# Layer 0's first attention heads: two of sixteen items begun inside the value projections

## What is computed

```python
s1 = jnp.einsum('bqhd,bkhd->bhqk', q1, k1).astype(jnp.float32) * scale
s2 = jnp.einsum('bqhd,bkhd->bhqk', q2, k2).astype(jnp.float32) * scale
a = jax.nn.softmax(s1, axis=-1) - lam * jax.nn.softmax(s2, axis=-1)
return jnp.einsum('bhqk,bkhe->bqhe', a.astype(v.dtype), v)
```

## Time and profile before

| | |
|---|---|
| median of 3 runs | 2467.47 us (2466.74 to 2468.09) |
| the profiled execution | 2467.12 us |
| its span, first to last instruction | 2465.3 us |
| TensorE busy | 2333.8 us, 95% of the span |
| VectorE / ScalarE / GpSimd busy | 1538.9 / 950.7 / 343.7 us |
| mean granted TensorE clock | 0.982 of full speed |

### The profile page before, as it was taken

One profiled execution on the slowest core, in us unless ns is written; L12 is line 12 of the kernel. 1 busy time (PEld: TensorE's weight loads), 2 busy tenths in 40 slices (PEclk: granted clock), 3 DMA queues, 4 the chain that ended last, 5 costly groups with the idle time before them and its releaser, 6 DMA issues.

```text
span 2465.3 us, 33152 instructions
## 1 busy us (share of the span) xinstructions
PE 2333.8 (95%) x13146; PEld 1893.8 (77%) x13146; DVE 1538.9 (62%) x2481; ACT 950.7 (39%) x1768; POOL 343.7 (14%) x455
## 2 busy tenths in 40 slices
PE   6989898999999899999999999999999999999997
PEld 3866566888887778777878787888887778788886
DVE  3647586666667652466778775655574667765457
ACT  4426453422212521476352232322342764433333
POOL 0110101101012210100100313133111110100131
PEclk9999999999999999999999999999999999999999
DMA  6430015654444222110412332333122104332221
GB/s 260 129 117 1 18 58 182 221 180 165 164 145 149 99 69 79 67 61 1 171 64 86 103 133 90 109 131 120 60 77 77 36 2 154 137 119 87 103 86 69
DMA packets 79178, 257.58 MB, mean 104 GB/s; under 512 B 5680, under 2 KB 10416, under 8 KB 70576
## 3 DMA queue, kind: packets, MB, share of 16 engines
q1 hardware_dynamic: 65024, 205.01, 24.2%
q0 software_dynamic: 12704, 46.14, 5.4%
q10 hardware_dynamic: 1296, 4.30, 0.4%
HBM read 246.00 MB, written 9.44 MB: 104 GB/s over the span
## 4 chain that ended last, share of the span: by engine, by line
PE 76%; DVE 12%; ACT 4%; issue 3%; DMA 2%; POOL 1%; SPq 1%; POOLq 0%; DVEq 0%; ACTq 0%
PE PS L1255 9%; PE PS L1257 9%; PE PS L1256 9%; PE PS L1326 5%; PE PS L1328 5%; PE PS L1327 5%; PE PS L1132 4%; PE PS L1151 3%; PE PS L1171 3%; PE PS L977 3%; PE PS L980 3%; PE PS L978 3%; PE PS L1025 1%; PE PS L1224 1%; PE PS L1227 1%
## 5 line engine op out<-in xcount | busy, mean ns | idle before, releaser
L1255 PE MATMUL PS<-HH,WH 128*128 128x512 f32 (+1 forms) x1088 | 420.4, 386 | 9.2 <-DVE TMP L2521 4.6
L1256 PE MATMUL PS<-HL,WH 128*128 128x512 f32 (+1 forms) x1088 | 416.7, 383 | 0.0
L1257 PE MATMUL PS<-HH,WL 128*128 128x512 f32 (+1 forms) x1088 | 416.7, 383 | 0.0
L2708 ACT ACTIVATE WH<-STG 128x1024 fp32r<-128x1024 f32 (+1 forms) x202 | 196.7, 1022 | 279.9 <-PE PS L1328 244.7
L2317 DVE TENSOR_TENSOR WL<-STG,WH 128x1024 fp32r<-128x1024 f32 (+1 forms) x202 | 241.6, 1237 | 36.9 <-ACT WH L2708 36.9
L1326 PE MATMUL PS<-WH,AH 128*128 128x512 f32 x600 | 238.0, 397 | 16.7 <-DVE LOW L2417 5.9
L1255 PEld LDWEIGHTS PS<-HH,WH 128*128 128x128 f32 x1088 | 204.5, 188 | 53.6 <-issue 5.7
L1328 PE MATMUL PS<-WH,AL 128*128 128x512 f32 x600 | 236.2, 394 | 0.0
L1327 PE MATMUL PS<-WL,AH 128*128 128x512 f32 x600 | 235.9, 393 | 0.0
L1257 PEld LDWEIGHTS PS<-HH,WL 128*128 128x128 f32 x1088 | 204.5, 188 | 40.3
L1256 PEld LDWEIGHTS PS<-HL,WH 128*128 128x128 f32 x1088 | 204.6, 188 | 40.0 <-issue 1.0
(11 more groups left out here) (268 smaller groups left out, 4464.5 us busy)
## 6 DMA issues: line engine op xcount, KB each, us to landing
STG<-in_w_up SPq DMA_DIRECT2D x66, 1024.0 KB, 6.0
ADAW<-in_w_ada SPq DMA_DIRECT2D x96, 512.0 KB, 3.8
STG<-in_w_down SPq DMA_DIRECT2D x20, 1024.0 KB, 5.7
ADAW<-in_w_ada POOLq DMA_DIRECT2D x32, 512.0 KB, 4.0
STG<-in_w_ffn_out SPq DMA_DIRECT2D x10, 1024.0 KB, 6.2
STG<-in_ev_w_in SPq DMA_DIRECT2D x8, 1024.0 KB, 5.0
STG<-in_w_in SPq DMA_DIRECT2D x6, 1024.0 KB, 6.9
spill<-X POOLq DMA_DIRECT2D x10, 512.0 KB, 5.1
```

The costliest lines, as they stand in the source:

```text
L1255: e.matmul(out, h_, hh, start=c == 0, stop=False)
L1256: e.matmul(out, h_, hl, start=False, stop=False)
L1257: return e.matmul(out, l_, hh, start=False, stop=c == 7)
L2708: return e.activation(dst, src, ACT.Copy)
```

## The change

- On TensorE the attention object is made before the projections. The second pair of values gets banks 4 and 5, the third 6 and 7, which leaves 0 to 3 to the scores. After the second pair TensorE waits for the last turned query and key (`keys_ready`) and does the scores of item 0; between the two halves of the third pair it does the scores of item 1. The loop starts at item 2, after the wait for the last value copy.
- VectorE does maxima and mix of items 0 and 1 after the second value pair, ScalarE their four exponentials, ahead of the copies of the third pair. Both loops start at item 2.
- Rows 0 to 3 go to X (`a_place`), since HT is still in use. Rows from 4 on keep their places in HT.
- `mix` takes both reciprocals of an item in one instruction over two columns; `total_inverse` is no longer called for A.
- VectorE's wait for the factor NLT moves ahead of the projections.

```diff
+    def a_place(self, n):
+
+        if n < 4:
+            o = (0, 768, 4096, 4864)[n]
+            return self.X[:, o:o + 768]
+        return self.att[0]["HT"][:, n % 6 * 768:(n % 6 + 1) * 768]
...
     def project(L):
         have, late = {v for v in range(2) if turned_ahead(L, v)}, []
         hh, hl = k.ht(L)
+        values = unit_pairs(0, 4) if L == 0 else []
...
+                if pair in values[1:]:
+                    rot["set"], rot["n"] = ([4, 5], [6, 7])[values.index(pair) - 1], 0
                 bs = [take(("proj", L, x[0])) for x in pair]
...
                         turn_late(L, late[:1] if kind == "qa" else late)
+                        if pair in values[2:]:
+                            first_heads.scores(1)
+                if pair in values[1:2]:
+                    keys_ready(0)
+                    first_heads.scores(0)
...
-        def turn(self, i, at, nkt, ready):
+        def scores(self, i):
+            QT, KT = k.reg(0, 0, 2048, 4), k.reg(0, 2048, 5120, 4)
+            h, c = i // 4, i % 4 * P
+            self.score_pair(i, [full_mm(QT[64 * s:64 * s + 64, h, c:c + P], KT[64 * s:64 * s + 64, h, :]) for s in range(2)])
+
+        def turn(self, i, nkt, ready):
             T = PS[:, 6:8, :].rearrange("p b n -> p (b n)")
-            Pt = self.HT[:, at * 768:at * 768 + nkt * P]
+            Pt = k.a_place(2 * i)
...
+    first_heads = PairAtt("A", 0, 6, 2)
...
-    scores_ready(0)
+    for x in values_done(k, 0):
+        w.wait_ge(*x)
...
-    for i in range(16):
...
+    for i in range(2, 16):
+        first_heads.scores(i)
         if i >= 3:
-            a.out_one(i - 3, lambda c, h=(i - 3) // 4: V[:, c, h * P:(h + 1) * P])
-        if i >= 2:
-            a.turn(i - 2, 2 * (i - 2) % 6, 6, k.dv_p(("A", i - 2)))
+            first_heads.out_one(i - 3, values_of(i - 3))
+        first_heads.turn(i - 2, 6, k.dv_p(("A", i - 2)))
...
@@ vector_program
                 step(bg, int(2 <= n < 10))
                 n += 1
+                if pair == unit_pairs(0, 4)[1]:
+                    for i in range(2):
+                        first_maxima(i)
+                        mix(i)
...
-        e.reciprocal(r2, tb).then_inc(*k.dv_rstd.up(("A", i, "r2")))
-        w.wait_ge(*k.dv_rstd(("A", i, "r2")))
+        both = k.small("att", 2 * i, 0, 8).rearrange("p (n j) -> p n j", n=2)
+        e.reciprocal(both[:, :, 2], both[:, :, 1]).then_inc(*k.dv_rstd.up(("A", i)))
+        w.wait_ge(*k.dv_rstd(("A", i)))
...
-    for i in range(18):
+    for i in range(2, 18):
         if i < 16:
-            w.wait_ge(*k.pe_score(("A", i)))
-            for n in (2 * i, 2 * i + 1):
-                largest("A", n, 768)
-        if 1 <= i <= 16:
+            first_maxima(i)
+        if 3 <= i <= 16:
             mix(i - 1)
-            total_inverse("A", 2 * (i - 1))
-        if i >= 2:
-            a_tail(i - 2)
+        a_tail(i - 2)
...
@@ scalar_program
+                if pair == unit_pairs(0, 4)[1]:
+                    w.wait_ge(*k.pe_turn((0, last_turn(0))))
+                    w.wait_ge(*k.pl_kr((0, 11)))
+                    for n in range(4):
+                        power("A", 0, n, 768, n)
                 late = pair
...
-    for i in range(16):
+    for i in range(2, 16):
         for n in (2 * i, 2 * i + 1):
-            if i >= 3:
+            if i >= 5:
                 w.wait_ge(*(k.dv_p(("A", i - 3)) if n % 2 else k.pe_pt(("A", i - 3, 1))))
```

More of the change, by code:

```diff
@@ L998, in project, with keys_ready @@
                 turn(L, x[0], *x[2:])
-    def scores_ready(L):
+    def keys_ready(L):
         us = [u for u, *_ in UNITS[L] if has_turn(L, u)]
@@ L1004, in scores_ready @@
         w.wait_ge(*k.dv_turned((L, [u for u in us if turned_by_dve(L, u) or UNITS[L][u][2] == "b"][-1])))
+    def scores_ready(L):
+        keys_ready(L)
         for s in values_done(k, L):
@@ L1420, in tensor_program, with values_of @@
     step(bg, 8)
-    a = PairAtt("A", 0, 6, 2)
-    QT, KT, V = k.reg(0, 0, 2048, 4), k.reg(0, 2048, 5120, 4), k.reg(0, 5120, 8192, 6)
-    for i in range(16):
-        h, tt = i // 4, LAT[i % 4]
-        a.score_pair(i, [full_mm(QT[64 * s:64 * s + 64, h, (tt - 2) * P:(tt - 1) * P], KT[64 * s:64 * s + 64, h, :])
-                         for s in range(2)])
+    V = k.reg(0, 5120, 8192, 6)
+    def values_of(i):
+        return lambda c: V[:, c, i // 4 * P:(i // 4 + 1) * P]
+    for i in range(2, 16):
+        first_heads.scores(i)
         if i >= 3:
-            a.out_one(i - 3, lambda c, h=(i - 3) // 4: V[:, c, h * P:(h + 1) * P])
-        if i >= 2:
-            a.turn(i - 2, 2 * (i - 2) % 6, 6, k.dv_p(("A", i - 2)))
-    a.out_one(13, lambda c: V[:, c, 3 * P:4 * P])
+            first_heads.out_one(i - 3, values_of(i - 3))
+        first_heads.turn(i - 2, 6, k.dv_p(("A", i - 2)))
+    first_heads.out_one(13, values_of(13))
     for i in (14, 15):
-        a.turn(i, 2 * i % 6, 6, k.dv_p(("A", i)))
-        a.out_one(i, lambda c: V[:, c, 3 * P:4 * P])
+        first_heads.turn(i, 6, k.dv_p(("A", i)))
+        first_heads.out_one(i, values_of(i))
     e.drain().then_inc(*k.pe_end.up("A"))
@@ L2111, in largest, with first_maxima @@
         e.tensor_reduce(k.small("att", n), k.scores(name, n)[:, 0:nk], AX.X, ALU.max, negate=True).then_inc(*k.dv_max.up((name, n)))
+    def first_maxima(i):
+        w.wait_ge(*k.pe_score(("A", i)))
+        for n in (2 * i, 2 * i + 1):
+            largest("A", n, 768)
     def lowest(s, table, start, out):
@@ L2127, in mix @@
     def mix(i):
[L2129 to L2132, removed]
+        ta, r2, rho = k.small("att", 2 * i, 1), k.small("att", 2 * i + 1, 2), k.small("att", 2 * i + 1, 3)
+        pa, pb = k.a_place(2 * i), k.a_place(2 * i + 1)
         w.wait_ge(*k.ac_exp(("A", 2 * i + 1)))
-        e.reciprocal(r2, tb).then_inc(*k.dv_rstd.up(("A", i, "r2")))
-        w.wait_ge(*k.dv_rstd(("A", i, "r2")))
+        both = k.small("att", 2 * i, 0, 8).rearrange("p (n j) -> p n j", n=2)
+        e.reciprocal(both[:, :, 2], both[:, :, 1]).then_inc(*k.dv_rstd.up(("A", i)))
+        w.wait_ge(*k.dv_rstd(("A", i)))
         e.tensor_scalar(rho, r2, ta, k.NLT[:, 0:1], ALU.mult, ALU.mult).then_inc(*k.dv_rstd.up(("A", i, "rho")))
@@ L2613, in vector_program @@
     bg = ada(1, 4)
+    w.wait_ge(*k.dv_lam("neg"))
     project(0, bg)
-    w.wait_ge(*k.dv_lam("neg"))
     def a_tail(i):
@@ L2872, in power @@
         w.wait_ge(*k.dv_max((name, n)))
-        e.activation(k.att[L]["HT"][:, at * 768:at * 768 + nk], k.scores(name, n)[:, 0:nk], ACT.Exp, bias=k.small("att", n),
+        dst = k.a_place(n) if name == "A" else k.att[L]["HT"][:, at * 768:at * 768 + nk]
+        e.activation(dst, k.scores(name, n)[:, 0:nk], ACT.Exp, bias=k.small("att", n),
                      scale=sign, accum_out=k.small("att", n, 1)).then_inc(*k.ac_exp.up((name, n)))
@@ L3164, in a_result @@
         w.wait_ge(*k.pe_out(("A", i)))
-        w.wait_ge(*k.dv_rstd(("A", 2 * i)))
+        w.wait_ge(*k.dv_rstd(("A", i)))
         copy(k.x(LAT[i % 4])[:, i // 4 * P:(i // 4 + 1) * P], k.result("A", i),
@@ L3169, in scalar_program @@
     w.wait_ge(*k.pe_proj((0, UNITS[0][-1][0])))
-    w.wait_ge(*k.pe_turn((0, last_turn(0))))
-    w.wait_ge(*k.pl_kr((0, 11)))
-    for i in range(16):
+    for i in range(2, 16):
         for n in (2 * i, 2 * i + 1):
-            if i >= 3:
+            if i >= 5:
                 w.wait_ge(*(k.dv_p(("A", i - 3)) if n % 2 else k.pe_pt(("A", i - 3, 1))))
@@ L3178, in scalar_program @@
                 a_result(i - 3)
-        if i >= 2:
-            a_head(i - 2)
+        a_head(i - 2)
     a_result(13)
```

## The result

| | before | changed |
|---|---|---|
| median (8 runs each) | 2467.18 us (2466.01 to 2472.59) | 2459.48 us (2457.31 to 2461.51) |
| profiled execution | 2467.12 us | 2458.89 us |
| its span | 2465.3 us | 2457.0 us |

The ratio of the times is 0.9968, 95% interval 0.9959 to 0.9977: 7.9 us less, 5.7 to 10.1. The forecast was 2460.0 us, 7.5 less. When the changed kernel was timed again later, on one chip with two others, the ratio was 0.9978 (0.9968 to 0.9987), 5.4 us less, and the medians were 4.3 us apart.

What follows compares the result with a forecast made beforehand. TensorE was taken to bound the kernel, idle then slow-clocked at attention A's start. Closing two gaps (5.6 us) and holding the clock (1.9) gave 7.5 us: 2467.1 to 2459.6, plus 0.35 for the median, 2460.0; range 2457.2 to 2463.4.

Steps and rivals of the forecast that it cites:

- Two groups in the projections: Scores of items 0 and 1 inserted into the value projections: 1.59 us each, 3.2 in all, bounds 1.4 to 2.0 each.
- Wait for the last copy: At the start of attention A's loop, item 2's scores still wait for the last value copy: 0.74 us as before.
- The two gaps: At attention A's start, gaps between score groups of 5.07 and 3.74 us replaced by 3.2 of inserted work: 5.6 gained.
- The clock: TensorE's granted clock no longer drops at 181 to 188 us, so two items avoid slow pace: 1.9 us.
- The reciprocal: One two-column reciprocal per item takes 16 instructions of 0.16 us off VectorE: 0 gain, bounds 0.1 either way.
- VectorE is not in the ring: VectorE waits 0.3 us for each score group in the 3.96 us item cycle, so fewer reciprocals gain 0.
- Slack of the second group: Item 1's scores come at 166.1, exponential 0 ends at 164.1: 2 us slack, covering the table load.
- Not given back: After the stage, weight loads near 400 us wait for VectorE and come forward too, so 7.5 us stays gained.
- A: Clock falls all the same in thinner TensorE work between 173 and 182: gain 5.6 us, 2461.9; chance 0.15.
- B: Inserted scores stall TensorE: up to 1.3 us for the second group, 0.8 for switches; gain 5.4, 2462.1; chance 0.06.
- C: Gain lost further on, a transfer setting the pace near 400 us, or queue order: gain 0 to 4, 2465; chance 0.05.
- D: Slower: half-array score groups inside value projections let the clock drop at 160; 17 us lost against 7.5, 2477; chance 0.02.

Runs made afterwards that it cites:

- the filled idle time: Kernel before, with five matmuls whose result nobody reads behind the first two score groups, nothing moved: stage 84.40 us, ratio 0.9995.
- two edits that keep the order of work: Kernel before with unread matmuls behind the first two score groups, stage 84.40 us; kernel before with the exponential table loaded after the second value pair, stage 83.14 us.
- the repeats: Both kernels executed again unaltered: stage 86.09 us for the kernel before, 78.89 and 78.90 us for the changed one.
- one item fewer: Changed kernel without item 1's scores in the third value pair, loops starting at item 1: stage 81.63 us, ratio 0.9981.
- two of the experiments: Changed kernel with only item 0 moved, stage 81.63 us; kernel before with the exponential table loaded after the second value pair, stage 83.14 us.
- the misplaced group: Changed kernel with item 1's scores directly behind item 0's instead of in the middle of the third value pair: stage 83.70 us.
- three items moved: Changed kernel with item 2's scores also in the third value pair and the last-copy wait behind item 3's scores: stage 77.37 us, ratio 0.9971.

## Why the prediction was right

**The sum.** Against T0, the forecast put the five score groups at 0.1, 7.0, 14.7, 18.4 and 22.4; they came at -0.2, 7.0, 14.9, 18.7 and 22.6. Term by term:

- Two groups in the projections: forecast 3.2 us. The last value copy starts 14.25 us behind T0 (160.87 to 175.12), for 10.82: 3.43. A group costs 1.7, not 1.59. Its 1.49 was right; the switches were read too low. The group starts 0.32 us behind the matmul before, and the first projection matmul behind it is followed after 0.33, each 0.1 over the usual pace. The transposes of the earlier trace rows had shown that only on the way out; on the way in they cost 0.02.
- Wait for the last copy: 0.74 forecast, 0.65 measured. Items 2 to 3: 3.72 and 3.83. Items 3 to 4: 3.96 and 3.90 (a wait on ScalarE that the change moves, see the end).
- The two gaps: forecast 5.6. Measured as the stage's 7.38 less 1.89 for the clock (the filled idle time): 5.5.
- The clock: 1.9 forecast, 1.89 and 1.87 shown by two edits that keep the order of work.
- The reciprocal: 0 forecast, 0.01 in the stage when done alone. The reason given, "VectorE is not in the ring", is loosely put: its maximum is in it, its reciprocals are not.
- Slack of the second group: 2.0 forecast, 2.2 measured.

**Not given back.** The stage's end came 7.38 us earlier and the second attention's first scores 8.12 (T0 + 129.96 before, 121.84 changed), since the fall of the clock behind the stage was shorter too. That last part is chance: the repeats have 129.19 before, 121.91 and 121.79 changed, 7.3 us and a little more. That transfers near 400 us keep step with VectorE was argued from the earlier trace rows, and no edit tested it by itself; the spans agree with it as far as their scatter lets them.

**Luck.** The whole came within 0.5 us of the forecast (2459.48 for 2460.0). The gain in the stage is what the prediction got right; that the total showed it so closely is chance. In the traced executions 1.8 us were lost ahead of the stage and 2.7 gained behind it, neither of them forecast, and in the second timing the medians are 4.3 us apart.

**The rivals.** A (the clock falls all the same, 0.15) didn't come in any of three executions. It was nearer than it looked: with one item fewer the clock did fall. The transposes of item 0 stood right before the idle 1.47 us, and the clock held at 1.00. The Trainium skill's page "TensorE: Matmul & The Clock Gate", in "Part 4: PE-mode transpose", says that transposes don't count as work for the clock as other matmuls do. By that rule TensorE was without counted work for 2.34 us there (scores of item 2 end at 177.26, item 3's start at 179.60), about as long as the idle spells in two of the experiments (2.27 with a fall, 2.23 and 2.17 without). So no row here needs the rule or refutes it, and the prediction's "speaks against it" says more than its rows carry. B was false: no wait before either group, and 1.7 us for each against the 2.0 of its bound. What a stall can cost there is shown by the misplaced group: 4.8 us, because the old gap and a slow clock return together, which the 2.1 given to B left out. C has nothing for it. D: 1.00 across the inserted groups.

**The range** of 2457.2 to 2463.4 was reasoned from a clock that moves by one stretch. Its terms (6.5 to 8.2 of gain, 1.8 to either side) give 2457.5 to 2462.8; the 0.3 and 0.6 beyond that have no term. Single runs of one kernel went from 2457.3 to 2465.0, so the width was about right for medians and too small for runs.

## What to carry to other kernels

Where a pipeline starts, ask what the first items need, and run them inside the last work that doesn't need their results; put the second item where the first one's chain is over, not right behind it. Price an idle spell of TensorE with the slow work behind it, and check by filling the spell with matmuls that nobody reads: it separates the clock from the order of work in one edit. For gains of 0.1%, measure between two fixed instructions of the stage; here these repeat to 0.2 us while the whole moves by 7.

## What the runs showed that I had not expected

- Loading the exponential's table early, one instruction, gives 3.15 us in the stage, where the whole change gives 7.38: 1.28 for the load, 1.87 since the clock then held.
- Two idle spells of 2.2 us (early table) left the clock at 1.00, one of 2.27 (one item moved) did not. What decides between them stays open.
- The interval from item 3 to 4 and 4 to 5 is 3.90 us in the changed kernel, then 3.96 as before. The first maximum there takes 0.99 us to the exponential's start (181.20 to 182.19) instead of 1.05. ScalarE's program has a likely cause: before each exponential it has one more wait from item 3 on in the kernel before, from item 5 on in the changed one (`if i >= 3`, now `if i >= 5`), from item 6 on with three items moved. The step from 0.99 or 1.00 to 1.05 comes at just these items in each: 182.13 is 1.00 behind its maximum and 187.28 is 1.05 in the kernel before, 186.10 is 0.99 and 190.06 is 1.05 in the changed one. No edit moved this wait alone. It makes 0.1 us, and it was no term of the prediction.
